# One layer of a hybrid attention and state-space trunk: small products laid out on array tiles, and the residual restored by another engine

## The chip, the core and the metric

The kernel runs on one core of a Trainium2 chip. The metric is the time of one execution on the device, in microseconds (us); lower is better. Engines are named as in the profile: PE is TensorE's matrix products and PEld its weight loads, DVE is VectorE, ACT is ScalarE, POOL is GpSimd, SP is SyncE, whose queue here issues nearly all DMAs.

## What is computed

16 meta tokens and 512 tokens of 1024 channels (L = 528 positions) pass through one layer. Both mixers read one normalised input:

```
xn = rmsnorm(h, norm1_g);  q, k, v, u, gates = split(xn @ w_in)      # 3 x 256, 512, 2 x 1024 columns
attn = stick_breaking_attention(rmsnorm(q), rmsnorm(k), v)            # 4 heads of 64, strictly causal
y    = s5_ssm(u)            # 32 groups of 16 channels, 64 complex states each: Re(C x) + D u
ssm  = g * sigmoid(g @ w_glu + b_glu),  g = gelu(y)
h    = h + (sigmoid(gate_a) * (attn @ w_attn_proj) + sigmoid(gate_s) * (ssm @ w_ssm_proj)) @ w_o
h    = h + (silu(conv_g) * conv_v) @ w_down,  conv = causal_dwconv(rmsnorm(h, norm2_g) @ w_up)
```

All is float32.

## The kernel before

**Units.** Everything large is a unit: 128 columns of a weight matrix times the whole sequence. A unit's weights are loaded by SP into `raw[slot]`, rounded by ACT into `hi` (`split`, L913), the rest taken by DVE into `lo` (`split`, L1296), and PE forms hi x xh + hi x xl + lo x xh (`three`, L1803). There are 104 units, two slots, two pairs of accumulation banks for them (0 to 3). Units 0 and 1 are plain float32 products on `hT`. While PE works on unit n, ACT and DVE split unit n + 2, and SP loads unit n + 2 when unit n's split is done. Units 0 to 3 give u, 4 and 5 k, 6 and 7 q, 8 and 9 v, 10 to 24 and 27 the gates, 25 and 26 the inner projection of the state-space output; 28 to 103 are the projections behind.

**Steps between units.** What is not a unit is a step, and a table written by hand, `STEPS`, says behind which unit each engine runs its part of it; `MOVES` says the same for SP's DMAs. Every engine goes through the table in order, so a step that waits on one engine holds up all that stands behind it there, the splits among it. ACT's `square` steps are run ahead of the unit's evacuation, all others behind the split.

**The state-space part** is cut into 4 rounds of 8 groups, and the sequence into 66 chunks of 8 positions. For a round r:
- POOL makes an input map (`input_map`, 6 operations of 128x512, or 12 of half that) into `g_in`, and POOL and DVE an output map into `hout` (`map_part`, L492 to L494, part 0 and part 1; 3 operations of 128x576 each).
- `prep` on PE transposes `g_in` (L1913) and forms the taps within a chunk from the output map (L1921); ACT copies both out (`win`, `kern`), DVE adds the direct term (L1491), SP spreads the taps over `toep` in 8 DMAs (`move_taps`, L533).
- `state` on PE forms each chunk's input (L1935); DVE rotates, scans and rotates back (L1512 to L1526) into `xst`.
- `readout` on PE adds `toep` x `uc` (L1947) and the output map x `xst` (L1952); ACT applies gelu into `yg`, SP writes it to DRAM.

`uc` is u by chunks, written to DRAM and read back (`u_write`, `u_read`). POOL's order is one list: input map 0, output maps 0 and 1, input map 1, output map 2, input map 2, output map 3, input map 3, then the attention's masks, then `hT` x `rb` for 8 tiles (L880), which gives back the residual that the first normalisation had scaled away; the residual is next read in unit 36.

**Attention.** `square`, `norms`, `scale` normalise q and k (sums of squares by PE with a selection matrix, L1904; a Newton step by DVE, L1302 to L1304), `turn_v` transposes v (L1966), `head` splits q and k of a head, `scores` forms the logits and adds the masks (L1987, L1998), then `suffix` and `values`.

**Who waits for whom in PSUM.** `used45` and `used67` hold the semaphore that says when banks 4, 5 or 6, 7 were last read; `prep`, `readout`, `norms` and `scores` wait on it.

```
def prep(r):                        # PE, before
    pe.wait_ge(g_ready, r + 1)      # POOL's input map
    ...
    pe.wait_ge(h_pool, r + 1)       # POOL's part of the output map
```

Of the kernel before, what the change touches and what calls it, by code (L numbers as in the profile page):

```python
# [17 lines left out]
F32 = mybir.dt.float32  # L18
# [26 lines left out]
T8 = 8  # L45
# [56 lines left out]
         3: [("turns", 0)], 4: [("columns", 1), ("turns", 1)],  # L102
         5: [("square", 0)], 6: [("square", 1)],
         7: [("square", 2)], 8: [("square", 3), ("prep", 0)], 9: [("state", 0), ("norms", 0)],
         10: [("prep", 1), ("out_map", 2)], 11: [("readout", 0), ("state", 1)],
         12: [("prep", 2), ("turn_v", 0), ("out_map", 3)] + [("scale", i) for i in range(4)], 13: [("readout", 1), ("state", 2)],
         14: [("prep", 3), ("turn_v", 1)], 15: [("readout", 2), ("state", 3)],
         16: [("readout", 3)],
# [18 lines left out]
NORM_ROWS = (0, 32)  # L127
TURN_BANK = (4, 4)
# [37 lines left out]
def hybrid_trunk(nc, x, meta_tokens, norm1_g, w_in, q_norm_g, k_norm_g, ssm_a_re, ssm_a_im,  # L166
# [3 lines left out]
    y_dram = nc.dram_tensor("y_dram", (SW, T8, NC), F32, kind="Internal").ap()  # L170
# [4 lines left out]
    with ctx:  # L175
# [37 lines left out]
        row_v, row_r, row_t = (sq[i][0:2 * NORM_ROWS[1], :] for i in range(3))  # L213
# [28 lines left out]
        uc = alloc(early, "uc", [P, 2, 2 * RP, NC])  # L242
# [6 lines left out]
        g_in = alloc(early, "g_in", [P, 2, RP, T8, GH])  # L249
# [8 lines left out]
        skip_i = alloc(early, "skip_i", [GH, GROUPS, GH])  # L258
# [111 lines left out]
        u_in = [sem(f"u_in{i}") for i in range(ROUNDS)]  # L370
# [94 lines left out]
        def turned_v(t):  # L465
# [74 lines left out]
        def _(sp):  # L540
# [1750 lines left out]
```

## Time and profile before

| | |
|---|---|
| median of 3 runs (lowest, highest) | 712.63 us (712.46, 713.18) |
| the profiled execution's own time | 712.44 us |
| its span, first to last instruction | 710.7 us |
| PE, DVE, ACT, POOL busy | 99%, 58%, 45%, 26% |
| DMA | 69.25 MB, 97 GB/s |
| mean granted clock of PE | 1.000 |

The profile is of one execution. The 1.7 us between its time and its span lie outside the first and last instruction. Engine shares are means over the whole program; the stretch that the change touches lies between 35 and 235 us.

### The profile page before, as it was taken

Reading aid. Unit: us, or ns where it says so; the run is one execution under the profiler, and the core shown is the slowest. Engines: PE = TensorE matmul, PEld = TensorE weight load, DVE = VectorE, ACT = ScalarE, POOL = GpSimd, SP = SyncE. Lnnn points to the kernel's source line nnn. Section 1 sums busy time; section 2 is a strip of 40 time slices with the busy share of each in tenths; the row PEclk is TensorE's granted clock in tenths of the full one; section 3 lists DMA queues with packets and bytes.
Section 4 is the critical chain, followed back from the end, with each engine's and each line's share of the span. In section 5 each row is a group of like instructions: output and inputs, shape, how many; then the busy total and the mean of one; then the engine's idle time right before and its main releaser. Section 6 shows DMA issues by size and latency. Waiting matters only on the chain.

```text
span 710.7 us, 13993 instructions
## 1 busy us (share of the span) xinstructions
PE 702.5 (99%) x5552; PEld 668.8 (94%) x5552; DVE 415.4 (58%) x557; ACT 319.7 (45%) x474; POOL 187.6 (26%) x215
## 2 busy tenths in 40 slices
PE   8999999999999999999999999999999999999998
PEld 7899899989999999999999999999999998888887
DVE  5764488867787756545765666666666662222221
ACT  4754343558888654435443444443343442211220
POOL 7899999940000022232011010101011010000000
PEclk9999999999999999999999999999999999999999
DMA  8163444545211233333333332323333343333331
GB/s 230 56 201 81 95 126 97 106 96 164 60 33 60 66 90 112 89 90 92 89 99 100 95 89 89 89 89 89 89 98 97 105 121 89 97 96 96 96 97 45
DMA packets 140520, 69.25 MB, mean 97 GB/s; under 512 B 24067, under 2 KB 138471, under 8 KB 140479
## 3 DMA queue, kind: packets, MB, share of 16 engines
q1 hardware_dynamic: 140319, 68.65, 35.0%
q8 instruction: 29, 0.48, 0.3%
q14 instruction: 12, 0.10, 0.0%
q10 hardware_dynamic: 160, 0.02, 0.0%
HBM read 63.19 MB, written 4.28 MB: 95 GB/s over the span
## 4 chain that ended last, share of the span: by engine, by line
PE 90%; DVE 3%; ACT 3%; SPq 1%; issue 1%; DMA 1%; POOL 0%; DVEq 0%; ACTq 0%
PE ps L1803 81%; PE ps L1987 1%; PE ps L2045 1%; PE ps L1854 1%; PE ps L1952 1%; PE ps L2012 1%; ACT xh L982 1%; SPq L626 1%; DMA xtok<-in_x_dram 1%; SPq L533 1%; ACT hi L913 1%; PE ps L1863 1%; PE ps L1921 1%; PE ps L1904 0%; PE ps L1947 0%
## 5 line engine op out<-in xcount | busy, mean ns | idle before, releaser
L1296 DVE TENSOR_TENSOR lo<-raw,hi 128x1024 fp32r<-128x1024 f32 (+2 forms) x102 | 136.5, 1339 | 152.6 <-ACT hi L913 152.3
L1803 PE MATMUL ps<-xh,hi 128*128 128x264 f32 (+1 forms) x1088 | 219.6, 283 | 0.1
L1803 PE MATMUL ps<-xl,hi 128*128 128x264 f32 (+1 forms) x1088 | 218.7, 282 | 0.0
L913 ACT ACTIVATE hi<-raw 128x1024 fp32r<-128x1024 f32 (+2 forms) x102 | 111.5, 1093 | 237.1 <-PE ps L1803 232.3
L1803 PE MATMUL ps<-xh,lo 128*128 128x264 f32 (+1 forms) x1088 | 217.9, 282 | 0.0
L1803 PEld LDWEIGHTS ps<-xh,hi 128*128 128x128 f32 x1088 | 167.2, 189 | 1.7 <-issue 0.8
L1803 PEld LDWEIGHTS ps<-xl,hi 128*128 128x128 f32 x1088 | 166.7, 188 | 0.0
L1803 PEld LDWEIGHTS ps<-xh,lo 128*128 128x128 f32 x1088 | 166.7, 188 | 0.0
L896 POOL TENSOR_TENSOR cv<-cv 128x512 f32<-128x512 f32 x22 | 28.4, 1289 | 226.7 <-DVE cv L1755 226.7
L1803 PE MATMUL ps<-ah,hi 128*128 128x512 f32 (+1 forms) x198 | 74.3, 375 | 0.0
L1803 PE MATMUL ps<-al,hi 128*128 128x512 f32 (+1 forms) x198 | 73.1, 369 | 0.0
L1803 PE MATMUL ps<-ah,lo 128*128 128x512 f32 (+1 forms) x198 | 73.0, 368 | 0.0
L1755 DVE SCALAR_TENSOR_TENSOR cv<-ut,cols,cv 128x512 f32<-128x512 f32 x88 | 65.9, 749 | 6.4 <-ACT cv L1241 0.9
L1744 DVE TENSOR_TENSOR ut<-ps,rb 128x516 f32<-128x516 f32 x44 | 30.6, 695 | 62.6 <-PE ps L1803 62.6
L883 POOL TENSOR_TENSOR ma<-ma,mb 128x516 f32<-128x516 f32 x8 | 10.9, 1358 | 126.8 <-DVE mb L1700 126.8
L1803 PEld LDWEIGHTS ps<-ah,lo 128*128 128x128 f32 x198 | 37.2, 188 | 7.3
L1803 PEld LDWEIGHTS ps<-al,hi 128*128 128x128 f32 x198 | 37.3, 188 | 6.6
L1803 PEld LDWEIGHTS ps<-ah,hi 128*128 128x128 f32 x198 | 37.2, 188 | 6.6
L1241 ACT ACTIVATE cv<-ut,cols 128x512 f32<-128x512 f32 x44 | 35.4, 805 | 1.7 <-DVE ut L1744 1.7
L1248 ACT ACTIVATE cv<-cv 128x512 f32<-128x512 f32 x22 | 13.9, 633 | 35.4 <-DVE cv L1755 35.4
L1803 PE MATMUL ps<-mh,hi 128*128 128x264 f32 (+1 forms) x128 | 25.7, 282 | 0.4 <-DVE ml L1684 0.3
L1803 PE MATMUL ps<-ml,hi 128*128 128x264 f32 (+1 forms) x128 | 25.8, 283 | 0.0
(291 smaller groups left out, 966.1 us busy)
## 6 DMA issues: line engine op xcount, KB each, us to landing
raw<-in_w_up_dram SPq DMA_DIRECT2D x88, 256.0 KB, 3.1
raw<-in_w_in_dram SPq DMA_DIRECT2D x52, 256.0 KB, 3.4
raw<-in_w_down_dram SPq DMA_DIRECT2D x16, 384.0 KB, 3.3
raw<-in_w_down_dram SPq DMA_DIRECT2D x16, 320.0 KB, 4.0
raw<-in_w_o_dram SPq DMA_DIRECT2D x16, 256.0 KB, 2.9
xtok<-in_x_dram SPq DMA_DIRECT2D x4, 512.0 KB, 5.7
raw<-in_w_ssm_proj_dram SPq DMA_DIRECT2D x8, 256.0 KB, 2.9
out_dram<-yt SPq DMA_DIRECT2D x7, 256.0 KB, 2.4
```

Of the source, the lines that this page charges most:

```text
L533: eng.dma_start(toep[p0:p0 + GH, :, GH * j:P], kern[:, :, 0:P - GH * j]).then_inc(kern_out[r], 16)
L626: sp.dma_start(uc[p0:p0 + GH, r % 2], src[j]).then_inc(u_in[r], 16)
L883: pool.tensor_tensor(ma[m % 2][:], ma[m % 2][:], mb[m % 2][:], ALU.add)\
L896: pool.tensor_tensor(cv[s][:, 1], cv[s][:, 0], cv[s][:, 1], ALU.mult)\
L913: act.activation(hi[slot][:, 0:n * P], raw[slot][:, 0:n * P], ACT.Copy)\
L982: act.activation(xh[:, k], hT[:, k], ACT.Copy, scale=g1[:, k:k + 1])\
L1241: act.activation(cv[s][:, part], ut[s][:, part, 2:2 + SEQ], ACT.Identity, bias=cols[:, bass.ds(m + COL_CB, 1)], scale=cols[:, bass.ds(m + ...
L1248: act.activation(cv[s][:, 0], cv[s][:, 0], ACT.Silu).then_inc(silu_a, 1)
L1296: dve.tensor_tensor(lo[slot][:, 0:n * P], raw[slot][:, 0:n * P], hi[slot][:, 0:n * P].bitcast(F32), ALU.subtract)\
L1744: dve.tensor_tensor(ut[s_][:, part], joined(4 * s_ + 2 * part, CUT_LATE), rb[:, 0:LL], ALU.mult).then_inc(up_v, 1)
L1755: dve.scalar_tensor_tensor(cv[s_][:, part], ut[s_][:, part, 2 + tap:2 + tap + SEQ], w, cv[s_][:, part], ALU.mult, ALU.add)\
L1803: ins = pe.matmul(o, weights[w], acts(a, c), start=start and i == 0, stop=stop and i == 2)
```

## The change

Seven things are changed.
- The products of `prep` on the output map alternate between PSUM partitions 0 and 64, those of `norms` go to four groups of 32 partitions, and those of `readout` on `xst` are cut into two of 64 output partitions each. ACT's copies of `kern` follow (4 of 256 columns for 2 of 512), and ACT's and DVE's work of `norms` is on 128 partitions for 36, with 4 DMAs of rows for 2.
- The input map has two buffers, `g_even` and `g_odd`; input map 1 is made in one piece.
- DVE makes part 0 of output maps 0, 1 and 2 (units 6, 7, 8), POOL part 1 of these and both parts of map 3, which now stands behind input map 3.
- The residual is restored by DVE (`restore`, in units 4 and 5) and no longer by POOL. `rms_write` and `rms_read`, which bring `rb`, go from units 7 and 8 to 2 and 3.
- `u_read` takes two rounds in one go, twice (8 DMAs of 16 x 16 x 66 elements each), in units 5 and 6; `uc` holds all four rounds. `y_write` is one DMA, `y_read` is 8.
- `turn_v` is in three steps (2, 4 and 4 transposes, units 10, 12, 14) in bank 7, and the next `readout` waits until DVE has read it.
- `head` 0 and 1 are steps of their own in units 15 and 16, and `scores` puts the mask products of a bank ahead of the others.

Cut to its core:

```diff
-STEPS = {... 4: [("columns", 1), ("turns", 1)], 5: [("square", 0)], 6: [("square", 1)], 7: [("square", 2)],
-         8: [("square", 3), ("prep", 0)], ... 10: [("prep", 1), ("out_map", 2)],
-         12: [("prep", 2), ("turn_v", 0), ("out_map", 3)] + scales, 14: [("prep", 3), ("turn_v", 1)], ...}
+STEPS = {... 4: [("columns", 1), ("turns", 1), ("restore", 0)], 5: [("square", 0), ("restore", 1)],
+         6: [("square", 1), ("out_map", 0)], 7: [("square", 2), ("out_map", 1)],
+         8: [("square", 3), ("out_map", 2), ("prep", 0)], ... 10: [("prep", 1), ("turn_v", 0)],
+         12: [("prep", 2), ("turn_v", 1)] + scales, 14: [("prep", 3), ("turn_v", 2)],
+         15: [("readout", 2), ("state", 3), ("head", 0)], 16: [("head", 1), ("readout", 3)], ...}
 # POOL
             input_map(0)
...
-            output_map(0, (0, 1))
+            output_map(0)
...
-            output_map(1, (0, 1))
+            output_map(1)
             input_map(1)
-            output_map(2, (1,))
+            output_map(2)
             input_map(2)
-            output_map(3, (1,))
             input_map(3)
+            output_map(3, (0, 1))
...
-            pool.wait_ge(rb_in, 16)
-            for k in range(KD):
-                pool.tensor_tensor(hT[:, k, :], hT[:, k, :], rb[:], ALU.mult).then_inc(h_raw, 1)
 # DVE
+            def restore(i):
+
+                dve.wait_ge(rb_in, 16)
+                dve.wait_ge(unit_done, U_PLAIN)
+                for k in range(i * KD // 2, (i + 1) * KD // 2):
+                    dve.tensor_tensor(hT[:, k, :], hT[:, k, :], rb[:], ALU.mult)\
+                       .then_inc(h_raw, 1)
 # PE, norms
-                        ins = pe.matmul(ps[rows, 6 + c, 0:w], sel[:, i], sq[i][:, c * w:(c + 1) * w],
-                                        start=i == 0, stop=i == 3, skip_group_check=True)
+                        ins = pe.matmul(ps[NORM_TILE * i:NORM_TILE * (i + 1), 6 + c, 0:HL],
+                                        sel[:, i], sq[i][:, c0:c0 + HL],
+                                        start=True, stop=True)
 # PE, prep
-                if r >= 2:
-                    pe.wait_ge(h_dve, r - 1)
-                for i in range(RP):
+                pe.wait_ge(h_dve, min(r + 1, HOUTS))
+                for k in range(RP // 2):
                     for c in range(2):
-                        ins = pe.matmul(ps[0:3 * GH, 6, i * P:(i + 1) * P],
+                        for half in range(2):
+                            i = 2 * k + half
+                            p0 = ST * half
+                            ins = pe.matmul(ps[p0:p0 + 3 * GH, 6, k * P:(k + 1) * P],
...
 # PE, readout
-                        ins = pe.matmul(group_out(g), hout[r % HOUTS][part, c, g // 2, 1:T8 + 1, :]
-                                        .rearrange("p i h -> p (i h)"),
-                                        xst[part, c, g // 2, :], start=False, stop=c == 1,
-                                        skip_group_check=True)
+                        maps = hout[r % HOUTS][part, c, g // 2, 1:T8 + 1, :]\
+                            .rearrange("p i h -> p (i h)")
+                        for half in range(2):
+                            mine = slice(ST * half, ST * half + ST)
+                            ins = pe.matmul(group_out(g)[mine], maps[:, mine],
+                                            xst[part, c, g // 2, :], start=False, stop=c == 1,
+                                            skip_group_check=True)
```

DVE's order from the split of unit 5 to that of unit 10, before (`lo<-raw,hi` is a split, `ct`, `rot`, `cols` are set-up, `kern` the direct term of round 0):

```order
L1296 TENSOR_TENSOR lo<-raw,hi 128x1024 x2
L1460 COPY cols<-ps 128x190
L1454 TENSOR_SCALAR rot<-rot 128x1056
L1296 TENSOR_TENSOR lo<-raw,hi 128x1024 x4
L1491 TENSOR_TENSOR kern<-kern,skip_i 16x8x16
```

and in the change (`hT<-hT,rb` is the restore, `gates<-pw,ct` begins an output map):

```order
L1307 TENSOR_TENSOR lo<-raw,hi 128x1024 x2
L1475 COPY cols<-ps 128x190
L1469 TENSOR_SCALAR rot<-rot 128x1056
L1676 TENSOR_TENSOR hT<-hT,rb 128x528 x4
L1307 TENSOR_TENSOR lo<-raw,hi 128x1024
L1676 TENSOR_TENSOR hT<-hT,rb 128x528 x4
L1307 TENSOR_TENSOR lo<-raw,hi 128x1024
L500 TENSOR_TENSOR gates<-pw,ct 128x576
L501 TENSOR_TENSOR mod<-pw,ct 128x576
L502 TENSOR_TENSOR gates<-gates,mod 128x576
L1307 TENSOR_TENSOR lo<-raw,hi 128x1024
```

Four restores now stand ahead of the split of unit 7 and four ahead of that of unit 8, and a part of an output map ahead of those of units 9, 10 and, by the third of them, the direct term.

PE's order between units 10 and 12, the units' own rows left out, before (`g_in` is the input map's transposes, `gates,bpair` the taps, `uc,toep` and `xst,gates` the readout, `uc,win` the state):

```order
L1913 MATMUL ps<-ident,g_in 128x128 x8
L1921 MATMUL ps<-gates,bpair 48x128 x8
...
L1947 MATMUL ps<-uc,toep 64x66 x16
L1952 MATMUL ps<-xst,gates 128x66 x16
L1935 MATMUL ps<-uc,win 64x66 x16
```

and in the change:

```order
L1931 MATMUL ps<-ident,g_odd 128x128 x8
L1941 MATMUL ps<-gates,bpair 48x128 x8
L1991 MATMUL ps<-ident,gates 128x128 x2
...
L1968 MATMUL ps<-uc,toep 64x66 x16
L1977 MATMUL ps<-xst,gates 64x66 x32
L1956 MATMUL ps<-uc,win 64x66 x16
```

Two transposes of v have come in behind the taps, and the products on `xst` are twice as many and half as wide.

## Rows read from the trace of the kernel before

**Rows 1.** The page, part 1: busy us (share of the span) of each engine.

```profile
PE 702.5 (99%) x5552; PEld 668.8 (94%) x5552; DVE 415.4 (58%) x557; ACT 319.7 (45%) x474; POOL 187.6 (26%) x215
```

**Rows 2.** The page, part 4: the chain that ended last, by engine.

```profile
PE 90%; DVE 3%; ACT 3%; SPq 1%; issue 1%; DMA 1%; POOL 0%; DVEq 0%; ACTq 0%
```

**Rows 3.** Timeline of PE, starts of units 7 and 8: start us, us, line.

```profile
63.59 0.40 PE L1803 MATMUL ps<-xh,hi 128*128 128x252 f32 x2
...
69.30 0.41 PE L1803 MATMUL ps<-xh,hi 128*128 128x264 f32 x2
```

**Rows 4.** Timeline of PE, small products, 75 to 157 us.

```profile
76.11 1.95 PE L1921 MATMUL ps<-gates,bpair 128*48 128x128 f32 x16
...
85.02 3.68 PE L1904 MATMUL ps<-gates,sel 128*36 128x264 f32 x16
...
103.26 1.16 PE L1947 MATMUL ps<-uc,toep 128*64 128x66 f32 x32
104.35 2.00 PE L1952 MATMUL ps<-xst,gates 64*128 64x66 f32 x32
106.28 1.20 PE L1935 MATMUL ps<-uc,win 128*64 128x66 f32 x32
...
132.92 1.09 PE L1913 MATMUL ps<-ident,g_in 128*128 128x128 f32 x8 [0.17 <-DVE mod L1513]
...
153.73 1.16 PE L1947 MATMUL ps<-uc,toep 128*64 128x66 f32 x32 [1.19 <-DVE xst L1526]
```

**Rows 5.** Single lines on PE: min/median/max ns of one record.

```profile
L1947 PE MATMUL ps<-uc,toep x128: 219/222/273, 103.3 to 154.7; 128*64 128x66 f32 x128
L1952 PE MATMUL ps<-xst,gates x128: 272/272/322, 104.4 to 156.5; 64*128 64x66 f32 x128
L1904 PE MATMUL ps<-gates,sel x16: 381/384/386, 85.0 to 88.3; 128*36 128x264 f32 x8, 128*36 128x258 f32 x8
```

**Rows 6.** Timeline of PE, scores of head 1.

```profile
181.27 0.29 PE L1987 MATMUL ps<-qh,k 128*128 128x272 f32 x1
...
182.78 0.37 PE L1987 MATMUL ps<-qh,k 128*128 128x272 f32 x1
```

**Rows 7.** Timeline of DVE, units 4 to 6, and two later operations of 128x528.

```profile
57.45 1.12 DVE L1454 TENSOR_SCALAR rot<-rot 128x1056 f32<-128x1056 f32 x1
...
59.73 2.25 DVE L1296 TENSOR_TENSOR lo<-raw,hi 128x1024 fp32r<-128x1024 f32 x1 [1.16 <-ACT hi L913]
...
65.38 1.61 DVE L1296 TENSOR_TENSOR lo<-raw,hi 128x1024 fp32r<-128x1024 f32 x1 [3.40 <-ACT hi L913]
...
113.69 1.10 DVE L1521 TENSOR_TENSOR mod<-mod,rot 128x528 f32<-128x528 f32 x1
...
135.19 0.71 DVE L1520 TENSOR_TENSOR mod<-mod,rot 128x528 f32<-128x528 f32 x1
```

**Rows 8.** DMA issues: KB each, median us from issue to landing.

```profile
rms_dram<-rt SPq DMA_DIRECT2D x1, 2.0 KB, 9.5
```

**Rows 9.** Timeline of SP's queue, load of unit 6.

```profile
43.91 0.92 SPq L549 DMA_DIRECT2D raw<-in_w_in_dram  x2
```

**Rows 10.** Timeline of DVE, ahead of readout 0, and in state 3.

```profile
100.06 0.27 DVE L1491 TENSOR_TENSOR kern<-kern,skip_i 16x128 f32<-16x128 f32 x1
...
148.38 1.56 DVE L1516 TENSOR_TENSOR mod<-mod 128x264 f32<-128x264 f32 x1
```

**Rows 11.** POOL by windows: us, busy (x), granted clock, DMA share, GB/s.

```profile
52.20:61.10 8.90, 8.25 (x6) 1.00 0.51 137
61.10:71.00 9.90, 9.37 (x6) 1.00 0.28 62
93.40:101.80 8.40, 7.87 (x6) 1.00 0.05 11
101.80:113.20 11.40, 10.36 (x12) 1.00 0.68 165
113.20:119.80 6.60, 6.01 (x6) 1.00 0.41 57
```

More of the change, by code:

```diff
@@ L101 @@
 STEPS = {0: [("angle", 0)], 1: [("angle", 1)], 2: [("columns", 0), ("angle", 2)],
[L102 to L108, printed above, removed]
+         3: [("turns", 0)], 4: [("columns", 1), ("turns", 1), ("restore", 0)],
+         5: [("square", 0), ("restore", 1)], 6: [("square", 1), ("out_map", 0)],
+         7: [("square", 2), ("out_map", 1)], 8: [("square", 3), ("out_map", 2), ("prep", 0)],
+         9: [("state", 0), ("norms", 0)],
+         10: [("prep", 1), ("turn_v", 0)], 11: [("readout", 0), ("state", 1)],
+         12: [("prep", 2), ("turn_v", 1)] + [("scale", i) for i in range(4)], 13: [("readout", 1), ("state", 2)],
+         14: [("prep", 3), ("turn_v", 2)], 15: [("readout", 2), ("state", 3), ("head", 0)],
+         16: [("head", 1), ("readout", 3)],
          17: [("scores", 0)], 18: [("suffix", 0)], 19: [("values", 0), ("scores", 1)],
@@ L212, in hybrid_trunk @@
         sq = [gates[:, 16 * LL - (i + 1) * L:16 * LL - i * L] for i in range(4)]
[L213 removed]
+        row_v, row_r, row_t = sq[0:3]
         hout_end = 16 * LL - 4 * L
@@ L289, in hybrid_trunk @@
         lal = alloc(heads, "lal", [P, SUM_COLS], F32R)
+        ql2 = [alloc(heads, f"ql2{i}", [P, LL], F32R) for i in range(2)]
         k2 = [alloc(heads, f"k2{i}", [P, L], F32R) for i in range(2)]
@@ L369, in hybrid_trunk @@
         u_out = [sem(f"u_out{i}") for i in range(ROUNDS)]
-        u_in = [sem(f"u_in{i}") for i in range(ROUNDS)]
+        u_in = [sem(f"u_in{i}") for i in range(2)]
         y_out = [sem(f"y_out{i}") for i in range(ROUNDS)]
@@ L672, in norm_read @@
                                      .partition_broadcast(DH)).then_inc(norm_in[i], 16)
-            move = {"norm_write": norm_write, "norm_read": norm_read, "rms_write": rms_write, "rms_read": rms_read, "u_write": u_write, "u_read": u_read, "toep": toep_move, "y_write": y_write,
+            move = {"norm_write": norm_write, "norm_read": norm_read,
+                    "rms_write": rms_write, "rms_read": rms_read, "u_write": u_write, "u_read": u_read, "toep": toep_move, "y_write": y_write,
                     "y_read": y_read}
@@ L989, in squares @@
                 act.wait_ge(drained, unit + 1)
+                if not is_k:
+                    act.activation(sq[i][:, LL:L], qT[:, t, 0:LATE0], ACT.Square)
                 act.activation(sq[i][:, 0:w], (kT if is_k else qT)[:, t, 0:w], ACT.Square)\
@@ L2058, in run @@
                     pe.wait_ge(masks_set, 4)
-                bank = {"turn_v": TURN_BANK}.get(name, (0,) * 4)[i]
-                if bank == 4 or name in ("prep", "state", "scores") or (name, i) == ("columns", 0):
+                if name in ("prep", "state", "scores") or (name, i) == ("columns", 0):
                     for s_, n in used45 if name != "scores" else ():
```

224 lines of the change are left out of this document (119 added, 105 removed).

## The prediction

> **What bounds the kernel now.** The page comes first: TensorE (PE) is busy for 702.5 of 710.7 us, VectorE (DVE) for 58% and GpSimd (POOL) for 26% [rows 1], and the granted clock is 1.00 in every window that I read [rows 11]. The chain that ended last is PE for 90% of the span, and no other engine has over 3% [rows 2]. So a microsecond counts where PE works it off or waits, and nowhere else. The timeline of PE in the stretch of the state-space work, 75 to 157 us, shows what is worked off there beside the projections [rows 4]: short groups of products between units of 5.7 us [rows 3], and one wait over 1 us, for `xst` ahead of the last readout, with 0.17 us at `prep` 3.
>
> **What a small product costs.** A float32 product leaves two records, so a group's pace is (row length less one record's own length) over (records less one). A record's own length is 0.22 us for L1947, 0.27 for L1952 and L1921 (the same 128 columns of one or the other operand) and 0.38 for L1904 [rows 5]; the groups' lengths are in [rows 4].
> - L1921 (48 columns, 128 moved): (1.95 - 0.27)/15 = 0.112 us a record.
> - L1904 (36 columns, 264 moved): (3.68 - 0.38)/15 = 0.220.
> - L1952 (64 rows, all 128 columns, 66 moved): (2.00 - 0.27)/31 = 0.056.
> - L1947 (64 columns, 66 moved, neighbours in different column halves): (1.16 - 0.22)/31 = 0.030.
>
> The last has the same 66 moved columns as L1952 and half its pace: products in different column halves do run side by side here. L1935 has two products in the same half, then two in the other, and still 0.032 a record ((1.20 - 0.22)/31). So a half does not wait for its turn in program order. I take it that each tile of the array works through its own records.
>
> **The change, part by part.**
> 1. *`prep`, L1921.* The two halves alternate. Two tiles: 16 records at 0.056 and not 0.112, 0.9 us saved in each of four rounds, **-3.6**. Bounds: 0 (no overlap), -3.6.
> 2. *`norms`, L1904.* Four column tiles of 32: 16 x 0.220 x 3/4 = 2.6 saved; 0.15 back for the array's change of tiling, between nothing and twice that. **-2.5**; only two tiles at a time gives -1.7.
> 3. *`readout`, L1952.* 16 products become 32 of half the width, in four quarters. By L1947, two tiles pass 0.030 a record; four give 0.015. 64 x 0.015 = 1.0 against 32 x 0.056 = 1.8: 0.8 saved a round, **-3.3**. If no more than two quarters run at once it is 64 x 0.030 = 1.9, +0.1 a round. I take four tiles, since L1952's own neighbours lie in different row halves and are at 0.056 with the full 128 columns to load; half the columns halved the pace in L1947.
> 4. *`scores`.* Five mask products a head move ahead of the others. The product behind a mask takes 0.37 us where its like takes 0.29 [rows 6]; two such places fewer are worth 0.1 a head, and `head` moved to units 15 and 16 takes ScalarE's (ACT's) and DVE's copies out of the way of the first suffix: **-0.6**, bounds 0 and -1.
> 5. *`turn_v`.* Ten transposes as before, now 2, 4, 4. Eight take 1.09 us at `prep` [rows 4], so the two in unit 10 cost 0.3 and the others get back 0.2: **+0.1**.
> 6. *Restore on DVE.* Eight multiplications of 128x528 leave POOL, where nobody waited for them, and stand ahead of the weight splits of units 5 and 6 on DVE. With two operands in SBUF one takes 0.71 us with POOL on short work and 1.10 with POOL in its maps [rows 7]; POOL is in its maps here, so 1.0. DVE is free at 57.45 + 1.12 = 58.6; four of them, 62.6; the split (1.6 to 2.25 [rows 7], say 1.7), 64.3. PE wants it at 63.6 [rows 3]: **+0.7**. The next four end at 68.3 and the split at 70.0, when PE, 0.7 late, wants it: 0. Bounds: none (0.71 each: the split is done by 63.1), and +2 (1.1 each, 2.25 for the split).
>
>    The Trainium skill (SBUF — State Buffer, "Who interferes with whom") says that a DVE instruction with two SBUF inputs contends with a GpSimd one that reads SBUF. The two rows agree, 0.71 against 1.10; a full lock by POOL's operations of over 1 us would give the +2.
> 7. *`rms_write`, `rms_read` earlier.* On SP's queue the read now waits in unit 3 for a landing of 9.5 us [rows 8]: written at about 36, landed at 45.5. The load behind it, issued at 43.9 before [rows 9], goes 2 us later; unit 6, which needs it, starts a unit ahead of 63.6 [rows 3], 12 us on: 0. `rb` lands by 51, ahead of 58.6.
> 8. *Output maps.* DVE takes one part of rounds 0 and 1 in units 6 and 7, and round 2 in unit 8, where it stood idle (3.4 us ahead of the split in unit 6 [rows 7]); round 3's goes to POOL. This puts the first `kern` addition 3.5 us later and eases DVE in units 10 and 12 by 3 us each, where `xst`'s chain runs. Cover: PE wants that round's taps some 14 us after.
> 9. *SP's queue.* `y_write` is one DMA and not 8, `u_read` 16 and not 32: some 20 us of issue less. No load was late for PE, so 0; `y_read` in 8 pieces costs SP 4 us in unit 19, with two units of slack. The second buffer of the input map frees POOL of a wait of which its rows show nothing: 0.
>
> **The waits that come instead.** PE gets to places earlier than the others.
> - *Readout 0* comes at 103.26 + 0.7 - 0.9 - 2.5 - 0.9 + 0.3 = 100.0. It now also waits for `turn_v` 0's low half, behind DVE's Newton steps, a split and `kern`: 100.06 + 0.27 [rows 10], and 0.5 for the copy: 100.8. **+0.8**. Neither Newton's nor the state's work on DVE gets shorter.
> - *`prep` 3* now needs both parts of output map 3 from POOL. POOL from 61.1: half of 9.9 for map 0, 1.0 for `decay`, 5.0 for map 1, 8.9 for a full input map, 8.4 for map 2, 11.4 and some 12 for two split input maps, then 2 x 6.6 to 2 x 8.4 [rows 11]: 126 to 130. PE wants it at 133.9 - 5.3 = 128.6: **+0.5**, 0 to 1.5. The old wait of 0.17 goes.
> - *Readout 3* waited 1.19 [rows 4] for state 3 on DVE. One operation in that chain took 1.56 with POOL restoring [rows 10], for 0.5 else. It shrinks by 0.7 (the last taps' DMAs then end near it).
>
> **Sum.** -3.6 - 2.5 - 3.3 - 0.6 + 0.1 + 0.7 + 0.8 + 0.5 - 0.2 - 0.7 = -8.8. The array's changes of tiling in `prep` and in `readout`, four of each, are in no row; 0.3 for them: **-8.5**. The profiled execution took 712.44 us (710.7 of it the span), so 703.9; the median of the runs is 712.63, 0.2 above it: **704.1**.
>
> **The rivals.**
> - *Two at a time.* If records start strictly in program order, the second record of a product waits for its first, and however many tiles there are, only two records overlap. Parts 2 and 3 then give 1.7 instead of 2.5 and -0.5 instead of 3.3; of the waits behind them 1.2 goes: 704.1 + 0.8 + 3.8 - 1.2 = 707.5. For it: no row shows more than two tiles. Against: L1935 in groups of two in the same half should run at 3/2 of L1947's time and runs at 1.05. Chance 0.18. The Trainium skill (TensorE: Matmul & The Clock Gate, "The mechanism") says that matmuls are "pc-monotone in start AND end — strict FIFO", which would make it this case; L1935's row speaks against it. The same page ("Measured speedup vs the span model") gives 10.6x for 16 tiles, which would not be had that way.
> - *DVE and POOL in each other's way.* With 1.5 us for each restore, as POOL's maps take, unit 7 waits to 66.8, 3.2 us, and unit 8 another 2.3; 1.3 of that is taken back at readout 0 and `prep` 3: 704.1 + 5.5 - 0.7 - 1.3 = 707.6. Chance 0.13.
> - *The tiles bring nothing.* Parts 1 and 2 at 0, part 3 at +0.1 a round; then PE is early nowhere and the waits are +0.7: about 712.5, no change. Chance 0.03.
> - *Slower.* Each quarter product of L1952 waits for the one before to leave the array, as products in one tile do: 64 records at 0.056 are 3.6 us for 1.9, +1.7 a round, +6.8, parts 1 and 2 bring nothing and the restore costs 0.7; less 1.3 for parts 4 and readout 3: 718.8. The sum passes zero where, with those two at nothing, a record takes over 0.033 us. Chance 0.03.
>
> **How the numbers follow.** Forecast 0.63, with a range of its own from 701.8 (no wait at units 7, 8 and `prep` 3, nothing for tiling changes, the whole of part 4) to 706. The range reaches to the two cases at 707.5 and a little on for both waits being larger: **701.8 to 709**, which leaves out some 0.1. A measurement of this kernel tells 0.2%, 1.4 us, from no change: faster 0.93, within it 0.04, slower 0.03.
>
> **What would show it.** Right: the products of `prep` 1.1 us a round, of `norms` 1.0 to 1.2, those on `xst` 1.1 with twice as many records; PE waiting under 1 us for `lo` ahead of unit 7, for DVE's `v` at readout 0, for POOL at `prep` 3. Wrong: products on `xst` still 1.9 us a round; restores of 1.5 us or more; a PE wait of over 2 us anywhere in 60 to 150 us; a projection unit after 160 us that no longer follows the last without a gap.

## The result

Forecast was 704.1 us; the changed kernel takes **715.4 us** (median of 16 runs, 714.9 to 718.0) beside 713.1 for the kernel before on the same chip: ratio 1.0036, interval 1.0026 to 1.0047. It is slower by 0.36%, a little more than the 0.2% that a measurement can tell, and outside the range of 701.8 to 709. One execution of `before_moves` below, 1142.8 us at a mean clock of 0.557, is left out of its median.

### The profile after

The page, parts 1, 2 and 4, beside [rows 1, 2]:

```profile
PE 698.6 (98%) x5680; PEld 665.4 (93%) x5680; DVE 427.7 (60%) x567; ACT 321.8 (45%) x483; POOL 170.7 (24%) x201
...
PEclk9989899999999999999999999999999999999999
...
PE 90%; DMA 3%; DVE 2%; ACT 2%; SPq 1%; issue 1%; POOL 0%; DVEq 0%; ACTq 0%
```

PE is busy 3.9 us less over a span 2.7 us longer (713.4 for 710.7), so it idles 6.6 us more. Two of the 40 slices show a granted clock below 0.9, and the chain has a DMA share of 3% in place of 1. The summed waits of PE say where (engine, tile, line, what it waited for: us in total, times, longest):

```profile
PE ps L1821 <- DVE lo L1307: 7.2, 2, 4.2
```

These are two waits for a weight split; the kernel before had neither. PE's timeline shows both, and the shapes that answer to [rows 4]:

```profile
50.08 0.81 PE L1821 MATMUL ps<-xh,hi 128*128 128x264 f32 x2 [4.18 <-DVE lo L1307]
...
73.83 0.80 PE L1821 MATMUL ps<-xh,hi 128*128 128x252 f32 x2 [2.98 <-DVE lo L1307]
...
88.31 1.04 PE L1931 MATMUL ps<-ident,g_even 128*128 128x128 f32 x8
89.28 1.08 PE L1941 MATMUL ps<-gates,bpair 128*48 128x128 f32 x16
...
97.49 1.10 PE L1921 MATMUL ps<-gates,sel 128*32 128x264 f32 x16
...
112.50 1.16 PE L1968 MATMUL ps<-uc,toep 128*64 128x66 f32 x32
113.58 1.17 PE L1977 MATMUL ps<-xst,gates 64*64 64x66 f32 x64
```

The three kinds of product are as forecast: 1.08 us for 1.95, 1.10 for 3.68, 1.17 for 2.00. But `prep` 0 begins at 88.3 and no longer at 75.1: **13.2 us are lost before the first merged product runs, and 10.5 gained behind it** (from the start of `prep` 0 to the end of the span, 713.4 - 88.3 = 625.1 us against 710.7 - 75.1 = 635.6). The forecast was +0.7 before it and -9.2 behind it.

**The first wait, 4.18 us ahead of unit 4.** The chain of the stretch 36 to 52 us, in order of time (start, us, what):

```profile
35.05 11.26 DMA u_dram<-uy
...
46.40 0.07 ACT uy L1152
...
47.52 0.86 ACT hi L923
...
48.47 1.56 DVE lo L1307
```

ACT may not copy unit 2's result into `uy` before the DMA of `u_write` 0 has read it, and ACT's `hi` and DVE's `lo` stand behind that copy. The DMA took 11.3 us. The DMA view of 33 to 50 us (KB each, median us from issue to landing), of the changed kernel:

```profile
raw<-in_w_in_dram SPq DMA_DIRECT2D x6, 256.0 KB, 7.0
u_dram<-uy SPq DMA_DIRECT2D x2, 264.0 KB, 10.2
```

and of the kernel before:

```profile
raw<-in_w_in_dram SPq DMA_DIRECT2D x9, 256.0 KB, 3.4
u_dram<-uy SPq DMA_DIRECT2D x3, 264.0 KB, 4.0
```

`u_write` takes two and a half times as long. The weights' 7.0 for 3.4 is less sure: with the same `rms_write` in the same place, rms_early below has 3.9 for them and 10.3 for `u_write`. The windows (us, busy of PE, PEld, DVE, ACT and POOL, granted clock, DMA share, GB/s) show the DMA engines as busy as before and moving little. The changed kernel:

```profile
40.00:47.00 7.00, 5.90 (x49) 5.68 (x47) 1.66 (x2) 0.60 (x2) 6.11 (x11) 1.00 0.62 54
47.00:50.00 3.00, 0.00 (x0) 0.00 (x0) 1.53 (x2) 1.37 (x3) 2.79 (x4) 0.84 0.71 180
50.00:58.00 8.00, 7.92 (x43) 7.93 (x44) 6.94 (x8) 6.22 (x7) 7.68 (x5) 0.63 0.39 119
...
74.00:80.00 6.00, 6.00 (x29) 6.00 (x30) 6.00 (x5) 0.00 (x0) 5.68 (x5) 0.52 0.31 87
```

The kernel before:

```profile
40.00:47.00 7.00, 7.00 (x60) 7.00 (x59) 5.83 (x9) 3.22 (x6) 6.35 (x8) 1.00 0.65 194
```

A share of 0.62 with 54 GB/s against 0.65 with 194. What is new in that stretch is `rms_write`: 528 elements of 4 bytes, issued right behind `u_write` 0. The trace of the kernel before holds the same harm where nobody waited for it: between 60 and 82 us, with `rms_write` in flight from 63, the weights' landing has a median of 6.1 us, for 3.4 over the whole program. And each of PE's waits is paid twice: behind the first the granted clock is 0.63 over 8 us, behind the second 0.52 over 6 us, nearly all of it at the lower of the clock's two levels (1.2 GHz and not 2.4).

**The second wait, 2.98 us ahead of unit 7.** DVE's timeline, beside [rows 7]:

```profile
65.14 6.60 DVE L1676 TENSOR_TENSOR hT<-hT,rb 128x528 f32<-128x528 f32 x4
71.66 2.12 DVE L1307 TENSOR_TENSOR lo<-raw,hi 128x1024 fp32r<-128x1024 f32 x1
73.70 6.37 DVE L1676 TENSOR_TENSOR hT<-hT,rb 128x528 f32<-128x528 f32 x4
```

Four multiplications take 6.60 us, so 1.65 each and not 1.0, and the split behind them is ready at 73.8. PE, 7.1 us late from the first wait, would have come at 70.85.

### The profile page after: what moved, and what is told of

It reads as the page before. It is cut to its first block, busy times and chain, and to the rows that moved or that the text cites. A ratio compares the mean times of both kernels' runs of the same rounds, so it can differ in the third digit from the quotient of the medians.

```text
span 713.4 us, 14228 instructions
## 1 busy us (share of the span) xinstructions
PE 698.6 (98%) x5680; PEld 665.4 (93%) x5680; DVE 427.7 (60%) x567; ACT 321.8 (45%) x483; POOL 170.7 (24%) x201
## 4 chain that ended last, share of the span: by engine, by line
PE 90%; DMA 3%; DVE 2%; ACT 2%; SPq 1%; issue 1%; POOL 0%; DVEq 0%; ACTq 0%
PE ps L1821 80%; PE ps L1881 2%; DMA u_dram<-uy 2%; PE ps L2074 1%; PE ps L2041 1%; PE ps L1872 1%; SPq L541 1%; PE ps L2024 1%; DVE hT L1676 1%; DMA xtok<-in_x_dram 1%; DMA raw<-in_w_in_dram 1%; ACT hi L923 1%; PE ps L1941 1%; DVE lo L1307 1%; PE ps L1931 0%
## 5 line engine op out<-in xcount | busy, mean ns | idle before, releaser
L1821 PE MATMUL ps<-xh,hi 128*128 128x264 f32 (+1 forms) x1088 | 222.3, 286 | 7.2 <-DVE lo L1307 7.2
L1821 PEld LDWEIGHTS ps<-xh,hi 128*128 128x128 f32 x1088 | 169.5, 191 | 9.1 <-DVE lo L1307 8.1
L1821 PEld LDWEIGHTS ps<-xl,hi 128*128 128x128 f32 x1088 | 168.9, 191 | 0.0
L1821 PEld LDWEIGHTS ps<-xh,lo 128*128 128x128 f32 x1088 | 168.6, 190 | 0.0
L1259 ACT ACTIVATE cv<-cv 128x512 f32<-128x512 f32 x22 | 13.9, 633 | 34.5 <-DVE cv L1773 34.5
```

The source lines that it names most:

```text
L1259: act.activation(cv[s][:, 0], cv[s][:, 0], ACT.Silu).then_inc(silu_a, 1)
L1821: ins = pe.matmul(o, weights[w], acts(a, c), start=start and i == 0, stop=stop and i == 2)
```

## The experiments

The theory: two losses ahead of `prep` 0, each a wait and then a stretch at the lower clock; A from the early `rms_write`, B from the restore on DVE. The rivals: other parts of the change cause them, or the place of the transfer and not its small elements, or the multiplication by itself and not POOL beside it. Each table row gives the median of all executions and the time of the profiled one, and splits the profiled one's span (1.7 us shorter than its time) at the start of `prep` 0. The split belongs to that one execution, which is not always near the median:

| kernel | median us | profiled us | to `prep` 0 | from `prep` 0 |
|---|---|---|---|---|
| before | 713.1 | 712.4 | 75.1 | 635.6 |
| changed | 715.4 | 715.1 | 88.3 | 625.1 |
| both_back | 708.0 | 708.9 | 75.7 | 631.5 |
| rms_early | 710.1 | 710.2 | 80.8 | 627.7 |
| rows_dve | 713.1 | 713.6 | 82.5 | 629.4 |
| late_dve | 708.1 | 708.0 | 75.1 | 631.2 |
| write_only | 714.0 | 712.8 | 81.5 | 629.6 |
| act_queue | 713.2 | 709.6 | 79.7 | 628.2 |
| before_moves | 727.1 | 725.1 | 88.1 | 635.3 |
| products | 713.1 | 715.3 | 75.7 | 637.9 |
| order_fix | 708.1 | 708.1 | 74.8 | 631.5 |
| order_fix2 | 709.1 | 706.9 | 76.7 | 628.5 |
| order_fix3 | 703.8 | 704.4 | 75.1 | 627.6 |
| after_orders | 714.9 | 715.0 | 88.4 | 624.9 |

### Both parts undone: both_back

```diff
- 2: [("u_write", 0), ("rms_write", 0)], 3: [("u_write", 1), ("rms_read", 0)],
+ 2: [("u_write", 0)], 3: [("u_write", 1)],
...
+ 7: [("rms_write", 0)], 8: [("rms_read", 0)],
...
- 4: [("columns", 1), ("turns", 1), ("restore", 0)], 5: [("square", 0), ("restore", 1)],
+ 4: [("columns", 1), ("turns", 1)], 5: [("square", 0)],
```

and POOL multiplies `hT` by `rb` behind its masks, as the kernel before does.

> The changed kernel with two of its parts undone: rms_write and rms_read stand in units 7 and 8 again, and GpSimd (POOL) restores the residual after its masks. The merged products and everything else stay. Theory: the changed kernel loses 13.2 us before `prep` 0, some 7.1 by the early rms_write (4.2 us of wait ahead of unit 4 and 2.9 at the lower clock behind it) and 6.0 by the restore on VectorE (DVE) (3.0 of wait, 3.0 of clock), and everything else gains 10.5: without the two parts 715.2 - 13.2 = 702.0, and back up to 1 us for waits that come nearer when PE is not late: 702 to 703.5. PE waits under 1 us between 36 and 85 us, clock 1.00 there. Rival (other parts of the change, the output maps on DVE in units 6 to 8 or the u_read in unit 5, cause a good part of it): over 705, and the waits ahead of units 4 and 7 remain in part.

Measured 708.0 us, ratio 0.9926 (0.9914 to 0.9938). The half about the first 85 us holds: no wait and full clock there, `prep` 0 at 75.7. The total misses by 5 us, for the part behind is 631.5 and not 625. (It lies where the rival had it, over 705, but the waits ahead of units 4 and 7 that the rival asks for are not there.) PE's timeline:

```profile
102.75 2.03 PE L1972 MATMUL ps<-uc,toep 128*64 128x66 f32 x32 [2.83 <-issue]
...
150.26 2.00 PE L1972 MATMUL ps<-uc,toep 128*64 128x66 f32 x32 [1.89 <-DVE xst L1544]
```

Readouts 0 and 3 wait 4.7 us where the changed kernel waits 0.2, and the same products then take 2.03 us for 1.16: the granted clock is 0.66 from 102 to 107 us. A PE that is 13 us late finds everything ready; one that is on time does not. So the two losses of 13.2 us cost 7.4 net, and the 10.5 us gained behind `prep` 0 were so many only because PE came late: on time it is 635.6 - 631.5 = 4.1.

### One loss at a time: rms_early, rows_dve, late_dve

rms_early takes back the restore alone:

```diff
- 4: [("columns", 1), ("turns", 1), ("restore", 0)], 5: [("square", 0), ("restore", 1)],
+ 4: [("columns", 1), ("turns", 1)], 5: [("square", 0)],
...
+ pool.wait_ge(rb_in, 16)
+ for k in range(KD):
+     pool.tensor_tensor(hT[:, k, :], hT[:, k, :], rb[:], ALU.mult).then_inc(h_raw, 1)
```

> Only the restore goes back to POOL; rms_write and rms_read stay in units 2 and 3. Theory: this leaves loss A alone: 702.5 + 7.1 = 709.6, with PE's wait of about 4 us ahead of unit 4 and none ahead of unit 7. Rival (the early move only hurts because DVE's restore follows it, or the wait ahead of unit 4 has nothing to do with the move): 702 to 704.

Measured 710.1 us, ratio 0.9975 (0.9959 to 0.9992); of 12 runs eight lie between 709.4 and 710.3, four between 712.7 and 715.0 at a mean clock of 0.992 to 0.995. A is there by itself: 3.88 us of wait at 49.6, clock 0.79 from 50 to 58, none ahead of unit 7; `prep` 0 at 80.8, 5.7 late.

```profile
49.59 0.51 PE L1824 MATMUL ps<-xh,hi 128*128 128x264 f32 x2 [3.88 <-DVE lo L1310]
...
106.44 1.16 PE L1971 MATMUL ps<-uc,toep 128*64 128x66 f32 x32 [1.48 <-issue]
```

rows_dve keeps both parts where the change has them and replaces the two transfers with one of whole rows. It leaves out the order of the residual's factors:

```diff
- sp.dma_start(rms_dram[0:META].unsqueeze(1), rt[0:META, 3, 0:1],
-              allow_slow_non_contiguous=True).then_inc(rms_out, 16)
- sp.dma_start(rms_dram[META:L].rearrange("(i p) -> p i", p=P), rt[:, 3, 1:NXT + 1],
-              allow_slow_non_contiguous=True).then_inc(rms_out, 16)
+ sp.dma_start(rms_dram[0:P * (NXT + 1)].rearrange("(p i) -> p i", i=NXT + 1),
+              rt[:, 3, :]).then_inc(rms_out, 16)
```

> The changed kernel as it is, but rms_write sends its 128 x 5 values as one transfer of 128 rows of 20 bytes, into a scratch tensor in another order, in place of 528 elements of 4 bytes each; what is left out is the order of the residual's factors. The move stays in units 2 and 3, the restore on DVE in units 4 and 5. Theory (many 4-byte packets hold up u_write and the loads behind them): 128 packets do a quarter of the harm or less, so the wait ahead of unit 4 falls under 1.5 us and only loss B is left: 702.5 + 6.0 = 708.5, at most 710. Rival (not the packets, but the place: any transfer to DRAM in front of u_write 1, or SP waiting for its landing): the wait of 4 us stays and the time is 714 to 716.

Measured 713.1 us, ratio 1.000 (0.9989 to 1.0011). The wait ahead of unit 4 is gone and `u_dram<-uy` lands in 4.0 us; so it is the form of the transfer, 528 elements of 4 bytes, and not its place. (The size of an element and the number of them change together here; no run tells the two apart.) B is left, and larger than I said: waits of 3.89 and 1.14 ahead of units 7 and 8, `prep` 0 at 82.5. The two by themselves, 5.7 and 7.4, make 13.1 of the 13.2. That they add up so well is partly luck: in the changed kernel the first takes 7.1 and the second 6.1, since PE comes late to the second. The time misses my 708.5 by B's size (7.4 for 6.0), by the 2.6 us that readout 0 waits again and by the clock.

late_dve has `rms_write` and `rms_read` in units 7 and 8 and the restore still on DVE:

```diff
+ 14: [("prep", 3), ("turn_v", 2), ("restore", 0)],
...
+ 26: [("restore", 1)]
```

> rms_write and rms_read back in units 7 and 8, and the restore stays on DVE, but in units 14 and 26, where POOL is idle and DVE has gaps of 4.5 us and over 2 us. Theory (a restore takes 1.6 us in units 4 and 5 because POOL works on its maps beside it): each takes 0.7 us here, PE waits nowhere for it, and the time is that of the kernel with both parts undone, or up to 0.7 us less, because POOL's restoring no longer slows the last state step on DVE: 701.5 to 703. Rival (the operation is slow by itself, whatever runs beside it): 1.5 us each, 6 us in unit 14 against a gap of 4.5, a wait of 1 to 2 us, over 704.

Measured 708.1 us, ratio 0.9939 (0.9926 to 0.9952). The single-line view of the restore (count: min/median/max ns):

```profile
L1677 DVE TENSOR_TENSOR hT<-hT,rb x8: 698/700/702, 135.7 to 238.9; 128x528 f32<-128x528 f32 x8
```

0.70 us where POOL has no maps to do, 1.65 where it has: what runs beside it is the cause. The Trainium skill (SBUF — State Buffer, "Who interferes with whom") calls the shared port pair an exclusive lock. 0.95 us more for each operation, beside POOL operations of 1.3 to 2.0 us, agrees with it in kind; a lock for the whole of both would give 0.70 and the 1.23 of a 128x576 map by itself, 1.93. POOL's slowdown of the last state step is gone too (readout 3 waits 0.4 for 1.9). Yet the time is that of both_back and not the 701.5 to 703 expected, for two reasons. The second half of the restore, in unit 26, does hold PE up: 2.56 us of it on DVE from 237.05 lead to a wait of 1.35 us for `sl` at 243.2, which both_back does not have. And readout 0 still waits:

```profile
102.22 1.91 PE L1969 MATMUL ps<-uc,toep 128*64 128x66 f32 x32 [2.90 <-issue]
104.07 1.96 PE L1978 MATMUL ps<-xst,gates 64*64 64x66 f32 x64
```

### What holds up the transfers: write_only, act_queue

Both start from rms_early. write_only puts `rms_read` back in unit 8:

```diff
- 3: [("u_write", 1), ("rms_read", 0)],
+ 3: [("u_write", 1)],
...
+ 8: [("rms_read", 0)],
```

act_queue issues the two writes from ACT's queue, ahead of unit 2's copy:

```diff
- 2: [("u_write", 0), ("rms_write", 0)],
+ 2: [("u_write", 0)],
...
+ def rms_write():
+     act.wait_ge(rms_set, 1)
+     act.dma_start(rms_dram[0:META].unsqueeze(1), rt[0:META, 3, 0:1],
...
+     act.dma_start(rms_dram[META:L].rearrange("(i p) -> p i", p=P), rt[:, 3, 1:NXT + 1],
...
  for unit in range(U_PROJ):
+     if unit == 2:
+         rms_write()
```

> As the kernel with the early rms_write and POOL restoring (710.1), but rms_read goes back to unit 8, so that SP never waits for the write's landing. Theory (the packets of 4 bytes hold up the u_write and the weight loads): the landing of u_write 0 and 1 stays near 10 us, the wait ahead of unit 4 stays at 3 to 4 us, 709 to 711. Rival (SP, waiting for the landing ahead of rms_read, issues its loads late, and this is what PE waits for): no wait over 0.5 us before unit 8, and 708 as with both parts undone.

> As the kernel with the early rms_write and POOL restoring (710.1), but the two transfers of rms_write are issued from ScalarE's own queue at the same time, about 36 us, not from SP's. Theory 1 (the small packets hold up what stands behind them in their own queue): u_write lands in about 4 us as before, PE does not wait ahead of unit 4, 708. Theory 2 (they hold up the 16 DMA engines, or the memory behind them, whatever queue they come from): u_write still takes 7 us or more and PE waits 2 to 4 us ahead of unit 4, 709 to 711. I give the second 0.6.

The DMA view of 33 to 50 us, of write_only:

```profile
raw<-in_w_in_dram SPq DMA_DIRECT2D x6, 256.0 KB, 6.0
u_dram<-uy SPq DMA_DIRECT2D x2, 264.0 KB, 10.8
```

and of act_queue:

```profile
raw<-in_w_in_dram SPq DMA_DIRECT2D x8, 256.0 KB, 4.3
u_dram<-uy SPq DMA_DIRECT2D x3, 264.0 KB, 9.3
```

PE waits 4.3 us ahead of unit 4 in the first and 3.1 in the second. SP's wait for the landing has no part in it; the queue from which the elements come matters little. The second agrees with a statement of the Trainium skill (DMA: Bandwidth & Descriptors, "Issuing engines are not separate DMA queues"), that all queues end at the same 16 engines. The same page ("Specifications") says that a transfer below 512 B is done as a read-modify-write; no run here shows that, and it can't be the whole of it, for the 20-byte rows of rows_dve fall under it too and hold up nothing. How the small elements hold the engines stays open. The times are 714.0 (708.5 to 715.4) and 713.2 (709.6 to 715.0), ratios 1.000 (0.998 to 1.002) and 0.999 (0.9975 to 1.0008). They lie 3 to 4 us over rms_early's, above what I expected of both, and spread over 5 to 7 us. In these two kernels the runs with the lower mean clock are the longer ones (write_only: 708.5 us at 1.000, 715.4 at 0.992), and most lie where four of rms_early's twelve do, 712 to 715 us. So the medians decide nothing here; the landings and the waits do. What A costs in time is as unsure: 2 us over both_back in rms_early, 5 to 6 in these two.

### The two losses without the gains: before_moves

The kernel before, with the changed kernel's `restore` on DVE in place of POOL's, and

```diff
- 2: [("u_write", 0)], 3: [("u_write", 1)],
- 7: [("rms_write", 0)], 8: [("rms_read", 0)],
+ 2: [("u_write", 0), ("rms_write", 0)], 3: [("u_write", 1), ("rms_read", 0)],
...
+ 4: [("columns", 1), ("turns", 1), ("restore", 0)], 5: [("square", 0), ("restore", 1)],
```

> The kernel before, with nothing but the two losing parts: rms_write and rms_read in units 2 and 3, the restore on DVE in units 4 and 5. Theory: here no gain brings PE early to the readouts, so nearly nothing of the two losses is made up behind them: 712.8 + 7.1 + 6.0 = 725.9, less readout 3's old wait of 1.2 and the 0.2 at prep 3: 724.5, at least 721. Rival (the losses cost net only what undoing them gave, 715.2 - 708.0 = 7.2): 720 or less.

Measured 727.1 us (725.1, 727.1 and 729.1), ratio 1.0206 (1.0185 to 1.0227), 2.6 over my 724.5. `prep` 0 begins at 88.1, and from there it takes 635.3 us, as before (635.6). Here, where nothing brings PE early, the losses cost their full 13 us: 12.7 in the profiled span, 13.9 by the medians.

### The gains without the rest: products

The kernel before with the products of `norms`, `prep` and `readout` alone:

```diff
+ ins = pe.matmul(ps[NORM_TILE * i:NORM_TILE * (i + 1), 6 + c, 0:HL],
+                 sel[:, i], sq[i][:, c0:c0 + HL],
...
+ for half in range(2):
+     mine = slice(ST * half, ST * half + ST)
+     ins = pe.matmul(group_out(g)[mine], maps[:, mine],
```

> The kernel before with the merged products of norms, prep and readout alone (and what they need in ScalarE's copies and the norms' rows); every step, transfer and map stays where it was. Theory A (the products save 2.6 + 3.5 + 3.3 = 9.4 us of PE's work, but PE then waits for the engines, whose work is no shorter: at prep 3 for the state's read on VectorE, which after the last output map and the scaling is free at 128.5 and has a split and two reads to do, 131.2, where PE comes at 127.6; and at readout 3, which waited 1.2 before): 712.8 - 9.4 + 3.5 + 1 to 2 for the clock, with one more microsecond at readout 3: 708 to 711, with PE's wait at prep 3 over 2 us. Theory B (nothing stands in the way in the old order): 703.4 to 705, no wait over 1.5 us.

Measured 713.1 us, ratio 0.9995 (0.9984 to 1.0005): no gain at all. PE's waits:

```profile
PE ps L1916 <- POOLq L823: 5.0, 2, 2.7
PE ps L1916 <- DVE mod L1516: 3.0, 1, 3.0
PE ps L1942 <- DVE v L1540: 2.0, 1, 2.0
...
PE ps L1976 <- ACT win L1017: 1.3, 2, 1.2
```

The wait at prep 3 is the 3.0 I expected; the 5.0 for POOL at preps 1 and 2 and the 2.0 at state 3 I had not seen. 11.3 us of waits take the place of 9.4 of work. In the old order POOL and DVE deliver each map just when PE came. The 5.0 us are for POOL's input maps, which stand behind its output maps: input map 1 is ready at 94.0 here and at 84.5 in both_back, where DVE has taken one part of output maps 0 and 1 (some 5 us each on POOL). In both kernels it begins 0.18 us behind the operation before it, so the second buffer has no part in that. The 3.0 us are for DVE, which here still does a part of output map 3 and then the scaling until 130.9. So the moved output maps, which I costed at nothing, let a good part of the gain through; how much, no run shows by itself, since both_back has the other steps of the change too. Its 631.5 from `prep` 0 and the 637.9 here also compare unlike runs: this profiled one is the longest of its twelve, 2.3 us over the median.

### Can the forecast be had? order_fix, order_fix2, order_fix3

All three start from late_dve. order_fix puts toep 0 behind the next weight load on SP, and DVE's Newton steps behind turn_v 0:

```diff
- 9: [("toep", 0)],
+ 10: [("toep", 0)],
...
-     if name in steps:
+     if name in steps and name != "norms":
+         steps[name](i)
+ if unit == 10:
+     norms(0)
```

> The kernel with the late restore on DVE (708.1), and readout 0's wait of 2.9 us attacked: on SP toep 0 goes behind the weight load of unit 12 and not ahead of it, and DVE does Newton's steps of the norms (3.3 us) behind the split, `kern` and turn_v 0 of unit 10, not ahead of them. Theory (with the two early losses gone PE comes to readout 0 at 99.3, and DVE, busy without a gap since 86.3, has turn_v 0's low half only at 102.1; the clock then falls for some 6 us, which costs 2.4 more): the low half is there by 98.5, PE does not wait, and 708.1 - 2.9 - 2.4 = 702.8, between 702 and 704. Rival 1 (the time lost there is made up behind: another wait, at prep 1's taps, at norms' scale in unit 12 or at readout 3, takes its place): 705 to 708, with that wait in the trace. Rival 2 (readout 0 waits for something else, the taps of toep 0): the wait stays or grows, 708 or more.

Measured 708.1 us, ratio 0.9928 (0.9912 to 0.9944). That is rival 1: readout 0 waits 0.2, readout 1 now 2.7.

```profile
99.25 1.16 PE L1971 MATMUL ps<-uc,toep 128*64 128x66 f32 x32 [0.20 <-issue]
...
119.49 2.03 PE L1971 MATMUL ps<-uc,toep 128*64 128x66 f32 x32 [2.70 <-DVE v L1551]
```

ACT's and SP's timelines of the same kernel tell whose wait it is:

```profile
116.51 1.53 ACT L1036 ACTIVATE kern<-ps 16x256 f32<-16x256 f32 x4 [5.37 <-DMA toep<-kern]
```

```profile
104.23 5.06 SPq L685 DMA_DIRECT2D gates<-norm_dram  x8
109.41 5.77 SPq L542 DMA_DIRECT2D toep<-kern  x8
```

order_fix2 exchanges those two on SP's queue:

```diff
- 12: [("norm_read", 0), ("toep", 1), ("y_write", 0)],
+ 12: [("toep", 1), ("norm_read", 0), ("y_write", 0)],
```

> The kernel before it moved the wait: readout 0 now waits 0.2 us, readout 1 waits 2.7, and its trace shows the chain: Newton's steps end 3 us later, so norm_write and norm_read go out 3 us later on SP, toep 1 behind them is issued from 109.4 to 115.2, and ScalarE's `kern` of round 2 waits for its landing (5.4 us). Here toep 1 goes ahead of norm_read on SP's queue. Theory: toep 1 is out by 110, `kern` 2 is copied by 113.5, turn_v 1's low half stands at 114.5, PE (116.8) does not wait at readout 1: 708.1 - 2.7 - 2 of clock = 703.4, between 702.4 and 704.6. Rival (a queue of waits: scale of the norms, 5 us later, or readout 2 or the first scores take it): 706 to 708.

Measured 709.1 us (6 runs, 706.9 to 709.7), ratio 0.9934 (0.9918 to 0.995). Readout 1 does not wait; prep 3 does, 1.62 us, for POOL. From `prep` 0 it takes 628.5, 3.0 less than order_fix, but its profiled run came to `prep` 0 at 76.7, 1.9 later, though nothing before that differs in the code: the granted clock from 15 to 21 us is 0.72 in it and 1.00 in order_fix, and the 16 plain products there take 5.48 us for 3.80. The theory's 703.4 fails, and a wait had stood behind the one removed, though not one that the rival named. The time, 709.1, is over the rival's 706 to 708 too: of the 3 us nothing shows in the median.

order_fix3 gives half of the last output map to DVE, where it stood idle 4.05 us:

```diff
- 12: [("prep", 2), ("turn_v", 1)] + [("scale", i) for i in range(4)],
+ 12: [("prep", 2), ("turn_v", 1)] + [("scale", i) for i in range(4)] + [("out_map", 3)],
...
- output_map(3, (0, 1))
+ output_map(3)
...
- pe.wait_ge(h_dve, min(r + 1, HOUTS))
+ pe.wait_ge(h_dve, r + 1)
```

> The second order kernel (toep 1 ahead of norm_read, 709.1 with 6 runs, 706.9 in the profiled one), whose only wait over 1 us behind unit 2 up to the scores is 1.62 at prep 3, for GpSimd's last output map. Here one of that map's two parts is done by VectorE in unit 12, behind the scaling, where it stands idle for 4.05 us (12 operations of GpSimd, 118.4 to 129.9, become 6). Theory: GpSimd is done by 125, prep 3 does not wait, 1.5 us less than the kernel before it: 705.3 to 707.6. Rival (VectorE's part takes over 4 us beside GpSimd's maps and the split of unit 14 goes late, and with it state 2's read): prep 3 then waits for VectorE, 1 us or more, and the time is that of the kernel before it.

Measured **703.8 us** (703.3 to 704.4), ratio 0.9867 (0.9853 to 0.9882), under my 705.3: **1.3% faster than the kernel before, 1.6% than the changed one.** Its page and its longest wait behind the first 33 us:

```profile
PE 693.8 (99%) x5680; PEld 660.5 (94%) x5680; DVE 427.0 (61%) x570; ACT 321.9 (46%) x483; POOL 167.8 (24%) x195
```

```profile
PE ps L1824 <- DVE sl L1664: 1.4, 1, 1.4
```

The wait for `sl` is the price of the late restore, as in late_dve. By the medians it is 5.4 us better than order_fix2, for one wait of 1.6; this I can't fully account for. The profiled runs differ by 2.5 (704.4 for 706.9), of which only 0.9 lies behind `prep` 0, where the edit is; the other 1.6 is order_fix2's late start of `prep` 0. The mean clock is 1.000 in all four runs of order_fix3, against 0.995 to 0.998 in order_fix2's six.

after_orders makes the edits of order_fix and order_fix2, and no other, in the changed kernel.

> The changed kernel with its two early losses left in, and the order edits alone (toep 0 and toep 1 earlier or later on SP's queue, Newton behind turn_v 0). Theory (the waits at the readouts are there only when PE is not 13 us late; in the changed kernel PE waits 0.2 us there in all): nothing is gained, 715.2, between 713.8 and 716.6. Rival (the order edits help by themselves, whatever comes before): 711 to 713.

Measured 714.9 us, ratio 1.0023 (1.0014 to 1.0033), beside 1.0036 for the changed kernel. As the theory has it: the order edits pay only where PE is not late.

## Why the prediction failed

- **Parts 1 to 3, the products: right.** 4 x 0.87 = 3.5, 2.6 and 4 x 0.83 = 3.3 us, for 3.6, 2.5 and 3.3. Four tiles at once was the right reading; the rivals "Two at a time", "The tiles bring nothing" and "Slower" fall by the rows at 89.28, 97.49 and 113.58.
- **Parts 4 and 5: too small to see.** From `prep` 0 to the end 10.5 us are gained; the products' 9.4, readout 3's wait (0.18 for 1.19) and prep 3's 0.17 make 10.6. Part 4's 0.6 is not to be found. The 0.15 and 0.3 us for changes of tiling stand in no row, and no run shows them by themselves; the groups' lengths hold what they cost, and with them the 9.4 is whole. The forecast for this part, -9.2, was missed by little, and by luck: the waits at readout 0 (+0.8) and `prep` 3 (+0.5) did not come because PE was 13 us late, and on time it gains 4.1 there (both_back).
- **Part 7 is the step that failed: "`rms_write`, `rms_read` earlier", costed at 0.** I took its landing of 9.5 us [rows 8] for the delay of what waits for it, `rb` and the next load. It is the mark of a transfer that keeps the DMA engines from others. What was late was `u_write`, which stands nowhere in that step, then ACT's copy, both splits, and PE by 4.2 us. The load behind it went out at 50.05, 6 us later than before and not 2. Price in place of 0: 7.1 us to `prep` 0 in the changed kernel, 5.7 alone (rms_early). No rival held it, and the trace of the kernel before would have shown it: weights landing in 6.1 us for 3.4 around its own `rms_write`.
- **Part 6 failed in size: 1.0 us a multiplication for 1.65.** The row of 1.10 [rows 7] is from 113.7 us, where POOL's operations are of 128x288; those beside the restore are of 128x576 and 128x512, and there it is 1.65 and 1.59. The rival "DVE and POOL in each other's way", with 1.5 us and 3.2 ahead of unit 7, had this right (2.98 measured, 3.89 in rows_dve) and got 0.13. It should have had more: the text itself named the lock.
- **A term that wasn't there: the clock.** Both waits were counted by their length alone. Behind each the clock fell to its lower level. The transposes of `columns` 1 come at 58.63 for 51.50 before, 7.1 late for a wait of 4.2, so 2.9 is the clock; of the rest, 13.2 - 7.1 - 3.0 = 3.1 is the clock behind the second.
- **"Readout 0" was forecast at +0.8**, and comes to 2.8 to 2.9 as soon as PE is on time (both_back, late_dve), with the clock behind it. The step let `kern` stay at 100.06 [rows 10]; in late_dve DVE works without a gap from 86.3 on, and the split ahead of `kern` (1.74 us for 1.21) and `kern` itself (0.72 for 0.27) run slower beside POOL, so the copy ends at 102.1 and not 100.8 (DVE is 0.6 us late there from 86.3 on); PE itself comes at 99.3 for 100.0. Without parts 6 and 7 the change takes 708.0, where the forecast without its +0.7 for them is 703.4: the sum would have missed by over 4 us even then.
- **Part 8, not in the sum, was right about the cost and saw half of the use.** It said that the moved maps ease DVE in units 10 and 12, and there `products`, without them, waits 3.0 us; that they bring POOL's input maps forward, worth 5.0 us of waits, it did not say. Without them and the other new steps the products bring nothing (products).

## What to carry to other kernels

A transfer whose landing is long for its size, here 2 KB in 9.5 us, may be more than a slow answer to one reader: look in the trace at what lands beside it, and put it where no other transfer is awaited; another queue did not help here. A microsecond of PE waiting costs more than one where the clock falls behind it: here waits of 3.0, 3.9 and 4.2 us cost 6.1, 5.7 and 7.1. And when work on the bounding engine gets shorter, go through the engines that feed it with the new times of arrival: in the old order the shorter products brought nothing, and only with the last of three order edits, each worked out from the wait that the one before had laid bare, was the forecast time reached (703.8 for 704.1).

## What the runs showed of the hardware

- 528 elements of 4 bytes written to DRAM stretch the landing of 264 KB transfers from 4.0 to 10.2 us, while the DMA share is 0.62 for 0.65 and the rate 54 GB/s for 194; issued from ACT's queue still 9.3; 128 rows of 20 bytes do nothing of the kind (4.0).
- A wait does not always bring the clock down: behind 2.98 us at 73.8 it was 0.52 for 6 us, while behind PE's wait of 3.00 us in products, at 135.1, the window of 130 to 137 us has 1.00, as has the one of 107 to 116 with a wait of 2.68. Nor is it the length: behind 1.89 us in both_back it is 0.72 from 150 to 156, behind 2.51 us in write_only 1.00 from 138 to 146. And the same kernel differs from run to run: the profiled run of products is the only one of twelve with a mean clock of 1.000 (the others have 0.995 to 0.998), and it is the longest. What tells the cases apart stays open.
- Products in four quarters of the array pass at (1.17 - 0.22)/63 = 0.015 us a record, half of two column halves [rows 4, 5]. (The 0.22 is the length of one record of L1977, 216 to 269 ns.)
- DVE's multiplication of 128x528 with both operands in SBUF takes 0.70 us by itself, 1.10 beside POOL's maps of 128x288 [rows 7], and 1.65 beside those of 128x576.
